# Expert weights of a mixture-of-experts stage: gate and up tiles loaded and given back in two halves

## The reference

```python
def moe_ffn(h, w_router, b_router, w_gu, b_gu, w_down, b_down):
    logits = (ht @ w_router + b_router)
    top_val, top_idx = lax.top_k(logits, TOP_K)          # 4 of 32 experts for each token
    gates = jax.nn.softmax(top_val, axis=-1)
    ...
    def expert_block(args):
        xblk, e = args
        hg = xblk @ w_gu[e] + b_gu[e]                    # 1,024 x 2,048 weights
        x_glu, x_lin = hg[:, :D_FF], hg[:, D_FF:]
        x_glu = jnp.minimum(x_glu, SWIGLU_LIMIT)
        x_lin = jnp.clip(x_lin, -SWIGLU_LIMIT, SWIGLU_LIMIT)
        act = x_glu * jax.nn.sigmoid(SWIGLU_ALPHA * x_glu) * (x_lin + 1.0)
        return act @ w_down[e] + b_down[e]               # 1,024 x 1,024 weights
```

## Time and profile before

| what | value |
|---|---|
| median of three runs | 2321.37 us |
| the profiled execution's own time | 2323.1 us |
| its span, first to last instruction | 2321.3 us |
| PE busy | 2219.7 us (96%) |
| DVE, ACT, POOL busy | 789.0, 372.4, 369.9 us |
| granted TensorE clock over the span | 0.988 of 2.4 GHz |
| moved by DMA | 602.76 MB, mean 260 GB/s |
| packets under 8 KB, of all | 146850 of 196206 |
| transfers of gate/up tiles, of down tiles | 256 and 128, 1024 KB each |

### The profile page before, as it was taken

One profiled execution on the slowest core, in us unless ns is written; L12 is line 12 of the kernel. 1 busy time (PEld: TensorE's weight loads), 2 busy tenths in 40 slices (PEclk: granted clock), 3 DMA queues, 4 the chain that ended last, 5 costly groups with the idle time before them and its releaser, 6 DMA issues.

```text
span 2321.3 us, 34149 instructions
## 1 busy us (share of the span) xinstructions
PE 2219.7 (96%) x11074; PEld 1272.1 (55%) x11075; DVE 789.0 (34%) x1709; ACT 372.4 (16%) x849; POOL 369.9 (16%) x2342
## 2 busy tenths in 40 slices
PE   6999999999999998999999899999899899999987
PEld 3464458888544677998888633333233233333323
DVE  1133655555560325884115321122121121111212
ACT  3222212111001312220224210010000010000001
POOL 0000020000001101000100033333233333333332
PEclk9999999999999999999999899999999999999999
DMA  9721342222584705557861399899999989989997
GB/s 381 248 74 55 104 133 91 91 91 82 174 269 146 236 1 182 164 165 260 283 211 61 146 382 422 354 423 422 383 397 422 422 357 422 422 358 422 422 422 289
DMA packets 196206, 602.76 MB, mean 260 GB/s; under 512 B 11042, under 2 KB 128034, under 8 KB 146850
## 3 DMA queue, kind: packets, MB, share of 16 engines
q1 hardware_dynamic: 193728, 599.04, 67.4%
q10 hardware_dynamic: 2402, 2.67, 0.4%
HBM read 600.62 MB, written 1.05 MB: 259 GB/s over the span
## 4 chain that ended last, share of the span: by engine, by line
PE 79%; DMA 12%; SPq 4%; DVE 2%; ACT 1%; POOL 1%; issue 1%; POOLq 0%; ACTq 0%; DVEq 0%
PE bank L371 52%; PE bank L964 26%; DMA wring<-in_w_gu 11%; SPq L2269 4%; DMA wring<-in_mod_w 1%; ACT big L1146 1%; POOL hT L2232 1%; DVE wring L1566 1%; PE bank L996 1%; ACT tmp L1146 0%; PE bank L989 0%; DVE big L1566 0%; DVE tmp L1566 0%; PE bank L677 0%; POOL xT L2259 0%
## 5 line engine op out<-in xcount | busy, mean ns | idle before, releaser
L964 PE MATMUL bank<-wring,big 128*64 128x512 f32 x3456 | 772.9, 596 | 41.1 <-DMA wring<-in_w_gu 32.7
L964 PEld LDWEIGHTS bank<-wring,big 128*64 128x64 f32 x3456 | 235.3, 137 | 529.4 <-issue 411.5
L371 PE MATMUL bank<-hT,wring 128*128 128x256 f32 (+2 forms) x1888 | 456.5, 396 | 8.3 <-POOL hT L2232 5.7
L371 PEld LDWEIGHTS bank<-hT,wring 128*128 128x128 f32 x1888 | 322.8, 193 | 125.1 <-issue 93.6
L371 PE MATMUL bank<-big,wring 128*128 128x256 f32 (+1 forms) x1096 | 344.7, 475 | 6.4 <-DVE big L1569 3.6
L2255 POOL COPY big<-hT 128x8 f32 x2240 | 306.7, 199 | 112.1 <-issue 112.1
L371 PEld LDWEIGHTS bank<-big,wring 128*128 128x128 f32 x1096 | 208.6, 191 | 138.9 <-issue 115.7
L371 PE MATMUL bank<-wring 128*128 128x256 f32 (+1 forms) x1408 | 245.9, 327 | 1.2 <-DVE wring L1566 1.1
L371 PEld LDWEIGHTS bank<-wring 128*128 128x128 f32 x1408 | 216.0, 191 | 20.3 <-DVE wring L1566 1.6
L1146 ACT ACTIVATE big<-bank 128x256 f32<-128x256 f32 (+3 forms) x239 | 89.5, 390 | 774.1 <-PE bank L989 385.4
L1569 DVE TENSOR_SCALAR big<-bank 128x512 f32<-128x512 f32 (+1 forms) x74 | 50.2, 678 | 447.2 <-PE bank L964 446.0
(11 more groups left out here) (169 smaller groups left out, 1240.5 us busy)
## 6 DMA issues: line engine op xcount, KB each, us to landing
wring<-in_w_gu SPq DMA_DIRECT2D x256, 1024.0 KB, 18.7
wring<-in_w_down SPq DMA_DIRECT2D x128, 1024.0 KB, 18.4
wring<-in_ffn_w_up SPq DMA_DIRECT2D x44, 1024.0 KB, 5.1
wring<-in_mod_w SPq DMA_DIRECT2D x24, 1024.0 KB, 15.5
wring<-in_mod_w SPq DMA_DIRECT2D x48, 512.0 KB, 4.4
wring<-in_ffn_w_down SPq DMA_DIRECT2D x16, 1024.0 KB, 5.6
wring<-in_w_ada SPq DMA_DIRECT2D x16, 1024.0 KB, 5.5
wring<-in_w_in SPq DMA_DIRECT2D x14, 1024.0 KB, 11.8
```

Of the source, the lines that this page charges most:

```text
L371: ins = pe.matmul(o, l, r, start=start, stop=stop, skip_group_check=True)
L964: ins = pe.matmul(o, l, r, start=start, stop=stop, skip_group_check=True)
```

## The change

Each gate/up tile comes as two transfers of 1,024 columns (4 KiB for each partition): the first raises `w_full` of the slot as before, the second a new semaphore `w_second` of the tile. PE waits for `w_second` before q = 2. `moe_used` is raised twice for a gate/up tile (after q = 1 and after q = 3; for tile 7 after q = 2 and by `token_ids`), so that an expert counts 20 (RING + GUC) instead of 12, and SP waits for each half by itself before it issues the transfer into that half. Down tiles are as before.

```diff
--- before.py
+++ after.py
@@ -179,6 +179,7 @@
         bank_full = [sem(f"bank_full{i}") for i in range(8)]
         bank_free = [sem(f"bank_free{i}") for i in range(8)]
         w_full = [sem(f"w_full{i}") for i in range(RING)]
+        w_second = [sem(f"w_second{i}") for i in range(GUC)]
         w_used = sem("w_used")
         names = {}
 
@@ -960,6 +961,10 @@
                 pe.wait_ge(w_full[i], e * 16 + 16 * (uses + 1))
                 return wring[:, i, :]
 
+            def wsecond(s, e):
+
+                pe.wait_ge(w_second[s], e * 16 + 16)
+
             def xmm(o, l, r, start, stop, inc=None):
                 ins = pe.matmul(o, l, r, start=start, stop=stop, skip_group_check=True)
                 if inc is not None:
@@ -1015,10 +1020,12 @@
                 for t in ts:
                     ws = wslot(t, e)
                     for q in range(4):
+                        if q == 2:
+                            wsecond(t, e)
                         inc = None
                         if t == 7 and q % 2:
                             inc = G("m_glu") if q == 1 else G("m_lin")
-                        elif t < 7 and q == 3:
+                        elif (t < 7 and q % 2) or (t == 7 and q == 2):
                             inc = G("moe_used")
                         elif t == 0 and q == 0:
                             inc = first
@@ -2310,24 +2317,32 @@
                     load_mod(k)
 
             def expert(s, e):
-                if s < GUC:
-                    return w_gu[0, e, P * s:P * s + P, :]
                 return w_down[0, e, 256 * (s - GUC):256 * (s - GUC) + 256, :].rearrange("(p j) n -> p j n", p=P)
+
+            def load_half(s, hf, src):
+                i = places[n0 + s][0]
+                sp.dma_start(wring[:, i, D * hf:D * hf + D], src).then_inc(w_second[s] if hf else w_full[i], 16)
 
             for s in range(RING):
                 wait_free(n0 + s)
-                load(n0 + s, expert(s, 0), SLOT)
+                if s < GUC:
+                    for hf in range(2):
+                        load_half(s, hf, w_gu[0, 0, P * s:P * s + P, D * hf:D * hf + D])
+                else:
+                    load(n0 + s, expert(s, 0), SLOT)
             sp.wait_ge(G("tables"), 1)
             with sp.Fori(1, NE) as turn:
                 done = sp.value_load(ends[0:1, bass.ds(turn - 1, 1)], min_val=0, max_val=MAXB - 2)
                 e = sp.value_load(turn_of[0:1, bass.ds(turn, 1)], min_val=0, max_val=NE - 1)
-                for s in range(RING):
-
-                    sp.wait_ge(G("moe_used"), done * RING + (s + 1))
-                    src = (w_gu[0, bass.ds(e, 1), P * s:P * s + P, :].rearrange("a p n -> p (a n)") if s < GUC else
-                           w_down[0, bass.ds(e, 1), 256 * (s - GUC):256 * (s - GUC) + 256, :].rearrange(
-                               "a (p j) n -> p j (a n)", p=P))
-                    load(n0 + s, src, SLOT)
+                for s in range(GUC):
+                    for hf in range(2):
+                        sp.wait_ge(G("moe_used"), done * (RING + GUC) + (2 * s + hf + 1))
+                        load_half(s, hf, w_gu[0, bass.ds(e, 1), P * s:P * s + P, D * hf:D * hf + D].rearrange(
+                            "a p n -> p (a n)"))
+                for s in range(GUC, RING):
+                    sp.wait_ge(G("moe_used"), done * (RING + GUC) + (GUC + s + 1))
+                    load(n0 + s, w_down[0, bass.ds(e, 1), 256 * (s - GUC):256 * (s - GUC) + 256, :].rearrange(
+                        "a (p j) n -> p j (a n)", p=P), SLOT)
             for c in range(DC):
                 sp.wait_ge(G("x_final") if c < DC - 1 else G("x_last"), c + 1 if c < DC - 1 else 1)
                 sp.dma_start(out[P * c:P * c + P, :], xT[:, c, 0:S]).then_inc(G("stored"), 16)
```

## The result

The changed kernel takes 2339.18 us, the median of four runs (2337.95 to 2341.72), beside 2321.40 us for the kernel before: a ratio of 1.0080, with a 95% interval of 1.0062 to 1.0097. It is slower by some 18 us; 11 were forecast. The profiled execution took 2341.72 us with a span of 2339.9, 18.6 us more than before's 2321.3.

What follows compares the result with a forecast made beforehand. DMA throughput was taken to bound the expert stage inside runs of transfers, PE only across pauses. Price + 19.0 less hand-over gain 7.9 made + 11.1 us, so 2332.5 us, 0.5% slower; range 2319 to 2341 us.

Steps and rivals of the forecast that it cites:

- What bounds the stage: Expert stage: five runs of transfers set by DMA throughput at 422 GB/s, with four 15.13 us pauses set by PE.
- Price of the pieces: Gate/up transfers in runs: 4 KiB pieces cost 0.079 us a tile, 240 tiles paying, + 19.0 us.
- Earlier hand-over: Pauses and run ends: 4 PE instructions fewer at each of nine places, 0.88 us each, 7.9 us gained.
- Waits, increments, issues: PE and SP: free inside a run; on the path nothing to 0.1 us a pause, 0.4 us at most.
- all of it on the path, since a run's length is its transfers' time: Runs of the expert stage: the whole 19.0 us price lengthens them.
- The forecast's own range: Whole kernel: 2325 to 2338 us, from a price of 0.05 to 0.10 us a tile.
- the wider one of 2319 to 2341: Whole kernel, us: range taking in most of the cancelled case and the missing gain.
- a rival at 0.06: Run starts or PE after tile 7: smaller first transfers start raggedly, gain missing, only + 19.0 left, 2340.4 us; chance 0.06.

Runs made afterwards that it cites:

- pieces: Kernel before with its whole 1,024 KB transfers, each gate/up transfer reading gate or up columns alone in 4 KiB pieces: 2350.94 us, ratio 1.0127.
- dense_halves: Changed kernel, but each half transfer reads 64 whole rows lying together, still in 4 KiB pieces (right weights left out): 2333.32 us, ratio 1.0051.
- dense_pieces: Kernel before with whole transfers, gate/up in 4 KiB pieces, each out of one 1 MiB stretch (right weights left out): 2339.92 us, ratio 1.0081.

## Why the prediction was right or wrong

**What bounds the stage**: right. Every kernel here is a sum of run lengths, pauses and an end, and its median moves with them to within 2 us (3.6 us in pieces).

**Price of the pieces**: right in kind and size for a full stretch, 0.075 us a tile against 0.079, 18.0 us of the 19.0; that the first expert's eight tiles are hidden fits all kernels whose gate/up tiles come in 4 KiB pieces but the changed one: the first run grew by 2.2 to 2.7 us (32 x 0.075 = 2.4; all 40 would be 3.0). The Trainium skill, "DMA: Bandwidth & Descriptors", section "Why small descriptors are slow (HBM only)", counts about 3 cycles for a packet, which was 0.03 us a tile. The trace doesn't agree: 0.075, and among the single packets of the changed kernel's middle stretch one of 4 KiB takes 159 ns at least and one of 8 KiB 309, so two of 4 KiB take 9 ns more, 3%.

**Earlier hand-over**: right at the places that it named. The pauses fell by 1.69 us (two times 0.88 forecast), the end by 0.84. Together -7.6 against -7.9 us.

**Waits, increments, issues**: right. On the path they are at most the 0.07 us by which a pause fell short of two times 0.88; nothing to 0.1 was forecast. SP's issues take longer more often (352 of 620 over 0.5 us, where it was 74 of 372), and halves land every 1.28 us all the same.

**The step that failed** is "all of it on the path, since a run's length is its transfers' time": the runs were to grow by 19.0 us and grew by 25.6. A run's length is its transfers' time and its start, and I let the start stand as it was, 3.5 to 3.7 us. It grew by 1.3 to 1.7 us in runs two to five, and the first run lost 1.4 us more at its second expert: 7.6 us in all, as much as the hand-over won. The forecast's own range, 2325 to 2338 us, does not hold the 2339.18; the wider one of 2319 to 2341 does, because it was stretched for the rivals, and that is luck as far as the mechanism goes. The start was in a rival at 0.06, with 2340.4 us, near the time measured; but its reason ("being smaller") is wrong. Small transfers that read rows lying together start no worse than whole ones in 4 KiB pieces (dense_halves beside dense_pieces), and whole transfers that read gate columns or up columns alone start as badly (pieces). The diff showed what was needed to ask: the slices `D * hf:D * hf + D` skip every second 4 KiB. The `mod_w` rows could not show it, as they were read only in full stretches.

What stays open is why packets of this pattern take longer only while a queue starts. The Trainium skill, "DMA: Bandwidth & Descriptors", section "Latency and other measured facts", reports copies between tensors in HBM that slow down where the rows of the partitions lie a large power of two apart (207 GB/s at 512 KiB and 103 at 4 MiB, 214 with a padded pitch), and calls the aliasing of lock-stepped streams an inference. Here pieces 8 KiB apart were slow, for some microseconds of a run; no run shows whether that is the same thing, nor the mechanism.

## What to carry to other kernels

When a transfer is cut, look at both what one piece costs in a full queue and what the first pieces read when the queue is empty: cut along rows that lie together, or issue the parts that fill each other's gaps one right behind the other (340 to 354 and 339 to 344 GB/s at the starts here, where the changed kernel has 312 to 321). Work out a stage's time as runs, pauses and starts, and check a gain at one of them against the other two, since here the gains at a pause, 0.65 to 1.7 us, were no larger than what a start can lose.

## What the runs showed that I had not expected

- The same 4 KiB pieces are read at 414 GB/s in a full stretch whether a transfer takes every second one or all that lie together, but at 311 to 326 against 337 to 365 GB/s over the first 15 us of a run (runs two to five of the changed kernel and pieces, and of dense_halves and dense_pieces).
- Every second 8 KiB costs nothing of the kind: 354 to 357 GB/s at the start, 422 in the middle.
- Pieces of 16 KiB for a third of the bytes lift a full stretch from 422 to 424 GB/s only.
